# Six copies on SyncE's queue and six accumulating DMAs on GpSimd's, into a DRAM scratch, in a three-block model kernel

## What is computed

```python
for l in range(DEPTH):                       # DEPTH = 2, the "layers"
    h = _rmsnorm(x, norm_g[l])
    p = _split(h @ w_in[l])                  # 19 projections
    ...                                      # MLA, differential, top-k and convolution branches
    x = x + y @ w_out[l]
x = _rmsnorm(x, final_g)
x = x + 0.5 * swiglu(rms_norm(x, g_ffn1), w_ffn1_gu, w_ffn1_down)   # first feed-forward
...                                          # mix, cross attention, second feed-forward
return rms_norm(x, g_final)
```

## Time and profile before

| | before |
|---|---|
| median of 2 runs | 1785.91 us |
| the profiled execution's span | 1785.4 us |
| PE busy | 1776.4 us, 99% |
| DVE busy | 1062.3 us, 59% |
| ACT busy | 750.5 us, 42% |
| POOL busy | 407.3 us, 23% (about half of each slice in the layers) |
| DMA | 165.53 MB, mean 93 GB/s |

### The profile page before, as it was taken

The page is one execution under the profiler, slowest core; times in us unless marked ns, Lnnn a source line. Parts: engine busy times, 40 slices in busy tenths (PEclk is TensorE's granted clock), DMA queues, the critical chain, the costliest instruction groups (busy, mean ns, idle before and its releaser), DMA issues.

```text
span 1785.4 us, 25187 instructions
## 1 busy us (share of the span) xinstructions
PE 1776.4 (99%) x9274; PEld 1437.2 (80%) x9274; DVE 1062.3 (59%) x2106; ACT 750.5 (42%) x1386; POOL 407.3 (23%) x248
## 2 busy tenths in 40 slices
PE   9999999999999999999999999999999999999998
PEld 7767778776777888888888878879888888888887
DVE  5888777588877665445433445555756654555333
ACT  6464654446454533223222455545444322232222
POOL 4544553455354310000000232220200200000000
PEclk9999999999999999999999999999999999999999
DMA  5422222322212343333333422323321333333332
GB/s 188 125 81 70 60 59 85 97 81 83 67 53 60 96 138 102 95 94 94 106 106 104 150 60 83 95 72 107 95 73 55 92 101 94 94 94 101 99 106 94
DMA packets 49765, 165.53 MB, mean 93 GB/s; under 512 B 5640, under 2 KB 6152, under 8 KB 49672
## 3 DMA queue, kind: packets, MB, share of 16 engines
q1 hardware_dynamic: 48376, 161.47, 30.2%
q10 hardware_dynamic: 1296, 2.84, 0.4%
HBM read 162.12 MB, written 2.17 MB: 92 GB/s over the span
## 4 chain that ended last, share of the span: by engine, by line
PE 97%; DVE 1%; ACT 1%; issue 0%; POOL 0%; DVEq 0%; POOLq 0%
PE proj L1013 78%; PE turned L1302 2%; PE o L1326 2%; PE score L1276 2%; PE turned L1530 1%; PE proj L1460 1%; PE o L1556 1%; PE score L1521 1%; PE proj L1453 1%; PE score L1285 1%; PE o L1652 1%; PE turned L979 1%; PE score L1641 1%; PE score L1163 0%; PE proj L991 0%; PE turned L998 0%
## 5 line engine op out<-in xcount | busy, mean ns | idle before, releaser
L1013 PE MATMUL proj<-hhi,whi 128*128 128x512 f32 x1456 | 580.2, 399 | 0.6 <-DVE tanh L2285 0.3
L1013 PE MATMUL proj<-hhi,wlo 128*128 128x512 f32 x1456 | 568.1, 390 | 0.0
L1013 PE MATMUL proj<-hlo,whi 128*128 128x512 f32 x1456 | 567.3, 390 | 0.0
L1736 ACT ACTIVATE whi<-ring 128x1024 fp32r<-128x1024 f32 x279 | 295.2, 1058 | 622.7 <-PE proj L1013 614.4
L2201 DVE TENSOR_TENSOR wlo<-ring,whi 128x1024 fp32r<-128x1024 f32 x199 | 243.1, 1222 | 164.8 <-ACT whi L1736 164.5
L1013 PEld LDWEIGHTS proj<-hhi,whi 128*128 128x128 f32 x1456 | 274.3, 188 | 59.4 <-issue 6.6
L1013 PEld LDWEIGHTS proj<-hhi,wlo 128*128 128x128 f32 x1456 | 273.4, 188 | 58.8
L1013 PEld LDWEIGHTS proj<-hlo,whi 128*128 128x128 f32 x1456 | 274.0, 188 | 52.8
L759 POOL TENSOR_TENSOR wlo<-ring,whi 128x1024 fp32r<-128x1024 f32 x80 | 194.7, 2435 | 372.6 <-ACT whi L1736 372.0
L771 POOL TENSOR_TENSOR prob<-prob 128x512 f32<-128x512 f32 x36 | 56.6, 1574 | 873.9 <-ACT prob L1732 873.9
L1762 ACT ACTIVATE prob<-prob,negmax 128x256 f32<-128x256 f32 (+3 forms) x208 | 114.4, 552 | 65.5 <-DVE negmax L2274 64.1
(11 more groups left out here) (334 smaller groups left out, 2426.1 us busy)
## 6 DMA issues: line engine op xcount, KB each, us to landing
ring<-wstream SPq DMA_DIRECT2D x287, 512.0 KB, 3.6
arena<-lines SPq DMA_DIRECT2D x28, 256.0 KB, 5.5
arena<-x ACTq DMA_DIRECT2D x4, 512.0 KB, 5.9
out<-arena SPq DMA_DIRECT2D x8, 256.0 KB, 2.9
arena<-mem SPq DMA_DIRECT2D x1, 1024.0 KB, 9.4
ring<-wstream ACTq DMA_DIRECT2D x2, 256.0 KB, 7.3
arena<-hot SPq DMA_DIRECT2D x2, 80.0 KB
par<-params ACTq DMA_DIRECT2D x2, 74.0 KB, 1.9
```

Source lines behind the costliest of these rows:

```text
L1013: mm = pe.matmul(b, rounded(w), rounded(rhs(v, k)), start=(first and n == 0 and p == 0), stop=(last and n == len(blocks) - 1 and p == 2))
L1736: act.activation(rounded(dst), src, ACT.Copy, scale=scale).then_inc(ready, 1)
```

## The change

A DRAM tensor `sums` of 18 blocks [128, 512] is added. In layer 0 SP issues a DMA after the loads at `i` = 12, 14, 16, 18, 20 and 22. Each copies, for three pairs of slots of the first feed-forward, the first quarter (512 words of a partition's row, by the width `4 * P`, the slot's first half) of the odd slot into three blocks of `sums`: 128 x 3 rows of 2 KB, 768 KB, from DRAM to DRAM. At the head of `layer(1)` POOL waits once for all six copies and then issues six DMAs of the same size, each of which adds the following 512 words of the same slots to the blocks (`accum_op=ALU.add`). SP waits at the very end until the six are done. Nothing reads `sums`. No instruction of PE, DVE or ACT is changed.

```diff
+N_PRE, PRE_STEP = 18, 3
...
+        sums = nc.dram_tensor("sums", (N_PRE, P, 4 * P), F32, kind="Internal").ap()
+        copied, added = sem("copied"), sem("added")
...
+            def quarter(first, slot, part):
+
+                at = (FFN1_AT + 2 * first + slot) * P * SLOT + part * 4 * P
+                return bass.AP(wstream.tensor, at, [[SLOT, P], [2 * P * SLOT, PRE_STEP], [1, 4 * P]])
...
                     if L == 0 and i == 3:
                         save_lines()
+                    if L == 0 and i in (12, 14, 16, 18, 20, 22):
+                        first = (i - 12) // 2 * PRE_STEP
+                        sp.dma_start(sums[first:first + PRE_STEP].rearrange("j p n -> p j n"), quarter(first, 1, 0)).then_inc(copied, 16)
...
+            sp.wait_ge(added, 16 * (N_PRE // PRE_STEP))
             sp.wait_ge(out_saved, 16 * 8)
...
             def layer(L):
+                if L == 1:
+                    for first in range(0, N_PRE, PRE_STEP):
+                        at = (FFN1_AT + 2 * first + 1) * P * SLOT + 4 * P
+                        src = bass.AP(wstream.tensor, at, [[SLOT, P], [2 * P * SLOT, PRE_STEP], [1, 4 * P]])
+                        pool.wait_ge(copied, 16 * (N_PRE // PRE_STEP))
+                        pool.dma_start(sums[first:first + PRE_STEP].rearrange("j p n -> p j n"), src, accum_op=ALU.add).then_inc(added, 16)
```

## The result

The changed kernel takes 1818.46 us (median of 2 runs, 1818.16 to 1818.76) against 1785.91 before: a ratio of 1.018, 95% interval 1.015 to 1.0209, 32.5 us slower. The forecast was 1829 us, within 1796 to 1858, with 0.61 on slower by more than 2%. It came out at 1.8%, with an interval up to 2.1%, so the data do not decide on which side of 2% it lies. The direction and the mechanism hold, and the size was 10 us too large: the median lies in the stretch from 1795 to 1821 us that was given 0.25, not in the main case from 1822 us up. The profiled execution's span is 1817.0 us, 31.6 us above that of before.

What follows compares the result with a forecast made beforehand. PE was taken as the only bound: 1785.4 us of span + 0 for copies + 41.4 of PE waiting (POOL held 51.4, less 10.0 of room) + 1.7 for the clock = 1828.5, so 1829 us, range 1796 to 1858.

Steps and rivals of the forecast that it cites:

- main case: Six additions at layer 1's head run one at a time, holding POOL 45 to 80 us: 1822 to 1858 us, chance 0.55.
- The bound: Whole run: PE works 1776.4 of 1785.4 us, so any microsecond PE waits lengthens the run and is never given back.
- The room on POOL, 10.0 us: Head of layer 1: POOL may be held 10.0 us after the root before PE waits for slot 4's low part.
- Lateness charged once: Layer 1: PE waits once, for slot 4's low part; slot 5's is made while PE works 5.6 us on CQ0.
- The copies at 0: SP's six 768 KB copies in layer 0 delay no ring load PE needs: 0 us; rival 16 us, chance 0.02.
- POOL's own time, 2.4 us: POOL's time to issue one accumulating DMA, taken from a pass over a slot: 2.4 us, from 0.33 to 4.8.
- Landing, 7.4 us after the issue: Each addition's time to land: 2.2 us fixed plus 48 x 0.109 us of packets, 7.4 us, from 4.3 to 10.0.
- B: Time the six additions hold POOL from the root's end at layer 1's head: six issues plus five landings, 51.4 us.
- The clock, 1.7 us: After PE's long wait the granted clock falls once to its lower level, losing 1.7 us of work, from 0 to 3.4.
- POOL is free as soon as a DMA is written: Rival at layer 1's head: POOL pays only six issues, 14.4 us, PE waits 4.4 us, 1786 to 1790 us; chance 0.11.
- Cheap ones in turn: Rival: additions one at a time, issue about 1.0 us, landing 4.3 us, 1803 us; chance 0.25 for 1795 to 1821.
- g: POOL's own time to issue one accumulating DMA at layer 1's head: taken as 2.4 us, from 0.33 to 4.8 us.

Runs made afterwards that it cites:

- the one with 2.7 us: All six additions spread one by one between POOL's other work of layer 1, against the kernel before the change: 1790.35 us, ratio 1.0019.

## Why the prediction was right, and where its size was off

- **The bound.** PE is the only bound, and a microsecond of its waiting is one of the run. Right: 31.0 us of wait and 2.2 us of clock are the difference (less the fall of 1.7 us that this execution does not have), and nothing was given back in some 1447 us of later work.
- **The room on POOL, 10.0 us.** Right to about 0.1 us, in seven kernels. It was read from one idle time of POOL (7.94 us) and the start of the job that needs the low part.
- **Lateness charged once.** Right: one wait in each trace; the second low part was made directly behind the first.
- **The copies at 0.** Right, by the kernel that has them alone. They land in 6.2 us, longer than a ring load, and the bursts of the earlier trace rows were a fair cover.
- **POOL's own time, 2.4 us.** This is the first mis-sized term: 1.2 us, since the price of a pass over a slot is not that of preparing a DMA. 6 x (2.4 - 1.2) = 7 us.
- **Landing, 7.4 us after the issue.** The second: 6.7 us, the mean of POOL's five idle times; it counts from the end of an issue to the next issue, where the 7.5 us of the page count from the start to the landing. The fixed part was right (2.1 against 2.2), and two reads in turn with the write beside them fit as well: 24 packets of 0.19 us, 4.6 us where 48 x 0.109 = 5.2 was taken, and 0.19 us for an added row is twice the 0.09 of a copied one. 5 x 0.7 = 3.5 us. Together 10.5 us, which is B: 51.4 forecast, 40.9 measured.
- **The clock, 1.7 us.** 2.2 us measured, after the wait. That a wait brings such a fall was a guess, and each kernel with a wait of 8.5 us or more had one, as had the one with 2.7 us. Two small things were not foreseen and nearly cancel by luck: the fall near 210 us is missing in the profiled execution (1.7 us less), and the median lies 1.5 us above the span, not 0.5.
- **The rivals.** "POOL is free as soon as a DMA is written" did not happen: POOL can't issue the next, and what stands behind that pays. By the sentence of the Trainium skill ("DMA: Bandwidth & Descriptors", "Issuing engines are not separate DMA queues") the time on the sequencer to start a DMA is usually small beside the DMA. The trace agrees for a single issue, 1.23 us of 7.5. "Cheap ones in turn" was the nearest in time (1795 to 1821), though with another make-up: not one read, but a shorter issue. That stretch got 0.25 and the main case 0.55, because the range of g was centred on the wrong row. The fit of the Trainium skill ("DMA: Bandwidth & Descriptors", Anatomy of one DMA), by estimate 3.8 us for such a size, was half of the 7.5 us that an addition took here, and below the 6.4 us of POOL's first plain copy between two DRAM tensors.

## What to carry to other kernels

Before several DMAs are put on GpSimd's queue, look at what stands behind the last of them on that engine and how long that may be late: here 10.0 us, less than two additions. With a scratch as small as here, reckon one issue plus one landing for each group of DMAs that go together, not one issue for each DMA, and do not cut DMAs smaller to make room, since every round pays the fixed part. If the transfers are not urgent, put one at a time where the engine is idle and the one before has landed; then they are free.

## What was not expected of the hardware

- POOL did not go on when the first of several DMAs in flight had landed, but when all had (pairs of copies: 332.9 landed, 335.6 resumed; triples of small additions: 334.3 and 338.0).
- Eighteen additions of 256 KB held POOL 48.9 us, nine of 512 KB 54.2 and six of 768 KB 40.9 for the same bytes. The middle size is worst: it went one at a time like the largest, and so paid the fixed part of a round most often.
- An addition takes 7.6 to 7.9 us from issue to issue when PE stands and no ring loads run, and 8.6 to 9.5 us beside them, and ring loads beside additions take 4.6 us instead of 3.6; the median of 3.6 over the whole run hides that.
- The granted clock fell to its lower level even behind a wait of PE of 2.7 us.
